# A scan-and-attention mixer: two drive steps set apart, one more PSUM bank in the ring, compressed scores by turns

## The chip, the cores and the metric

The kernel runs on one core of one Trainium2 chip. The metric is the time of one execution on the device, in microseconds (us). The engines are named as the profile names them: PE is TensorE's matmul (PEld its weight load), DVE is VectorE, ACT is ScalarE, POOL is GpSimd, SP is SyncE, which here only issues DMAs. L571 is line 571 of the kernel before.

## The reference

Two blocks over 512 tokens of width 1024, all in float32. The first block is an FFN, then a mixer, then a second FFN and a gated addition; the second block has two layers of its own, which the change leaves alone. The change lies in the mixer, and from one input projection the mixer makes two things:

```python
z = rmsnorm(h, norm_mix) @ w_in
q, kc, vc, ksl, vsl, kw, vw, g, u = split(z)
# attention, 8 heads in 2 groups, query blocks of 128
p_cmp = masked_softmax(q @ compress(kc).T * scale)     # 31 compressed keys
p_slc = masked_softmax(q @ ksl.T * scale)              # 8 blocks, all selected
p_win = masked_softmax(q @ kw.T * scale)               # window 512
o = g0 * (p_cmp @ vc') + g1 * (p_slc @ vsl) + g2 * (p_win @ vw)
# S5: 32 groups of 64 complex states, a linear recurrence over the 512 tokens
state[t] = a_bar * state[t-1] + b_coef * (B @ u[t])
y = gelu(Re(C @ state) + d * u);  out = y * sigmoid(y @ w_glu + b_glu)
h = h + concat(o, out) @ w_out
```

## The kernel before

Each engine runs its own program, in order, and semaphores join them. Activations lie transposed, with features on the 128 partitions and 512 tokens along the free dimension. Weights come by DMA from SP into three slots (`RAW`), in a fixed order in which a load waits until the tile three places ahead in that order has been used. Most weights are split in two halves: ACT writes the high one (`WHI`, L1109), DVE the low one (`WLO`, L1580), and PE multiplies three products.

**The mixer's order.** One generator, `mix_order` (L210), yields steps, and PE, ACT, DVE and POOL each walk the whole list and do their own part of a step. So one list sets the order on all of them. It goes through the four `u` projections, then eight `qk` projections with rotation (`rope`, `turn`) and the compression matmuls (`squeeze`), then eight `v` steps, then 34 rounds n of attention. In round n stand `values` of an earlier group, `flip` of scores n-2 (transposes, L785), `scale` of n-1, `scores` of n, for the first rounds also `squeeze` and `weigh`, and then two steps of the S5 generator `s5_order` (L191). In the `qk` part three S5 steps follow each projection, in the `v` part one.

**The S5 steps.** The 16 state tiles are worked in 8 batches b of two tiles j.
- `drive` b, j: PE makes the real and the imaginary input (two matmuls of 32 rows into two PSUM banks, L571); DVE makes four products with the rotation tables (L1796 to L1800; each has one PSUM input); POOL makes two additions (L2217, L2219).
- `scan` b, c, chunk c of 0 to 3: DVE runs four scans of 128 columns (L1816) and, between chunks, two small carry operations (L1821, L1823). The first scan needs POOL's additions of the drives of its batch.
- `back` b, j: one product on DVE (L1583) and three on POOL (L2230, L2232, L2234). They need the last scan of b, POOL's additions of `drive` b+1, j, since they write the same temporary buffers, and `read` b-1.
- `read` b: PE multiplies the eight results (L571, tiles of 32 columns), the last of them after POOL's last product of `back` b, 1; DVE adds into `U` (L1583, 64 partitions).

Before the change the order within a batch is: scans 0 to 3 of b, `read` b-1, `drive` b+1, 0, `drive` b+1, 1, `rest` (nothing), `back` b, 0, `back` b, 1.

**PSUM banks.** `take` pops the bank at the head of a list, `ring`, and makes PE wait until the last user of that bank has read it; `give` puts it at the tail with the name of that reader. Seven of the eight banks are in the ring; the eighth, `STAT`, is used only by `colsum`, the column sum of a normalization, of which the mixer's is read by DVE before the first `u` is stored. `squeeze` holds two banks over four steps, `v` four over eight, and `values` one over many rounds.

**Attention, each round.** PE writes two score tiles (one per key group, rows 0 to 63 and rows 64 to 127 of the array), DVE takes the row maximum (L1906), ACT the exponential (L1274), DVE the reciprocal and the gate (L1912, L1915), ACT the scaled copy (L1282), PE transposes (L785), ACT copies (L1290). `weigh` 0 to 3 are the compressed scores: per key group four matmuls of 31 columns with 64 rows (L571), and an addition of the mask on DVE (L1877). `weigh` 4 to 6 are their softmax.

Of the kernel before, what the change touches and what calls it, by code (L numbers as in the profile page):

```python
# [14 lines left out]
P = 128  # L15
# [175 lines left out]
def s5_order():  # L191
    for b in range(-1, 9):
        if 0 <= b < 8:
            for c in range(4):
                yield "scan", b, c
        if b >= 1:
            yield "read", b - 1
        if b + 1 < 8:
            yield "drive", b + 1, 0
            yield "drive", b + 1, 1  # L200
        if 0 <= b < 8:
            yield ("rest",)
            yield "back", b, 0
            yield "back", b, 1

# [90 lines left out]
def program(nc, D, out):  # L296
    ctx = ExitStack()
    with ctx:
# [78 lines left out]
        P_, A, V, G = Sig(sem("s_pe_done")), Sig(sem("s_act_done")), Sig(sem("s_dve_done")), Sig(sem("s_pool_done"))  # L377
# [6 lines left out]
        def loaded(name):  # L384
            if name not in X:
                X[name] = Sig(sem("s_" + name), 16)
            return X[name]
# [48 lines left out]
        ring = []  # L436

        def take(pe, *name):

            b, sig, by = ring.pop(0)  # L440
            if sig is not None:
                pe.wait_ge(*sig.at(*by))
            bank_of[name] = b
            return PS[b], b

        def give(b, sig, *by):
            ring.append((b, sig, by))
# [28 lines left out]
        Q = ar(13312, 4, T)  # L476
# [6 lines left out]
        KCC = ar(18816, 64)  # L483
# [82 lines left out]
        def pe_program(e):  # L566
            pe = PE(e)
            ring[:] = [(b, None, ()) for b in range(7)]

            def mm(o, l, r, start, stop):  # L570
                return pe.matmul(o, l, r, start=start, stop=stop, skip_group_check=True)  # L571
# [24 lines left out]
            def colsum(st):  # L596
                pe.wait_ge(*G.at("sq", st, 7))
                pe.wait_ge(*loaded("consts").at())
                mm(STAT[:, :], ONES, ACC, True, True).then_inc(*P_.up("colsum", st))

            def ffn(z):
# [45 lines left out]
            for step, *at_ in mix_order():  # L647
                if step == "u":
                    give(w_in(at_[0]), V, "u", at_[0])
                elif step == "rt":  # L650
                    ps, b = take(pe, "rt")
                    pe.wait_ge(*V.at("rs", "mix"))
                    for j in range(4):
                        t = pe.transpose(ps[:, P * j:P * j + P], RS[:, P * j:P * j + P], IDENT)
                    t.then_inc(*P_.up("rt"))
                    give(b, A, "rt")
                elif step == "drive":
                    b, j = at_
                    t16 = 2 * b + j
                    y4, r = t16 // 4, slice(32 * (t16 % 4), 32 * (t16 % 4) + 32)  # L660
# [8 lines left out]
                elif step == "read":  # L669
                    b, = at_  # L670
                    y4, r = b // 2, slice(64 * (b % 2), 64 * (b % 2) + 64)
                    ps, bY = take(pe, "read", b)
                    for z in range(4):
                        for j in range(2):
# [3 lines left out]
                            if z == 0:  # L678
                                pe.wait_ge(*V.at("back_im", t16))
                                t = mm(o, CpR[:, t16, :], S5T[k2], True, False)  # L680
                            elif z == 1:
                                pe.wait_ge(*G.at("back_re", t16))
                                t = mm(o, CpI[:, t16, :], S5T[k1], False, False)
                            elif z == 2:
                                pe.wait_ge(*G.at("back_vr", t16))
                                t = mm(o, CpR[:, t16, :], vr, False, False)
                            else:
                                pe.wait_ge(*G.at("back_vi", t16))
                                t = mm(o, CpI[:, t16, :], vi, False, True)
                    t.then_inc(*P_.up("read", b))  # L690
                    give(bY, V, "read", b)
                elif step == "qk":
                    i, = at_
                    b = w_in(4 + i)
                    give(b, V, *(("vct",) if i == 1 else ("rope", i)))
                elif step == "turn":
                    i, = at_
                    ps, b = take(pe, "turn", i)
# [3 lines left out]
                elif step == "squeeze":  # L702
                    z, c = at_
# [6 lines left out]
                    for mt in range(2):  # L710
                        for i in range(4):
                            ii = 4 * c + i
                            t = mm(hc_banks[z][mt][0][:, 0:62], w[:, i, P * mt:P * mt + P],
                                   XBp[:, ii, :, :].rearrange("p g c -> p (g c)"), ii == 0, ii == 15)
# [4 lines left out]
                elif step == "compressed":  # L719
                    z, = at_  # L720
                    ps, b = take(pe, "compressed", z)
                    pe.wait_ge(*A.at("hidc", z, 1))
                    pe.wait_ge(*loaded("small_w").at())
                    if z == 0:
                        for mt in range(2):
                            t = mm(ps[:, 0:62], WK2[:, mt, :], HIDc[:, mt, 0:62], mt == 0, mt == 1)
                    else:
                        for g in range(2):
                            for mt in range(2):
                                t = mm(ps[0:31, 64 * g:64 * g + 64], HIDc[:, mt, 31 * g:31 * g + 31], WV2[:, mt, :], mt == 0, mt == 1)  # L730
                    t.then_inc(*P_.up("compressed", z))
                    give(b, A, "compressed", z)
                elif step == "v":
# [6 lines left out]
                    for k in range(4):  # L740
# [6 lines left out]
                        t = mm(o, xl, hi[:, k, :], False, kk == 7)  # L747
# [4 lines left out]
                        give(v_banks[tt][1], A, "gx", tt)  # L752
                elif step == "weigh" and at_[0] < 4:
                    qt, = at_
                    for hf in range(2):
                        ps, b = take(pe, "weigh", qt, hf)
                        r = slice(64 * hf, 64 * hf + 64)
                        pe.wait_ge(*G.at("turn", 7))
                        pe.wait_ge(*A.at("compressed", 0))
                        for i in range(4):  # L760
                            t = mm(ps[:, 32 * i:32 * i + 31], Q[r, i, P * qt:P * qt + P], KCC[r, 31 * hf:31 * hf + 31], True, True)
                        t.then_inc(*P_.up("weigh", qt, hf))
                        give(b, V, "weigh", qt, hf)
                elif step == "scores":
                    i, kind, qt = at_
                    nk = P * (qt + 1)
                    keys = KSL if kind == 1 else KW
                    bs = [take(pe, "scores", i, kind, qt, hf) for hf in range(2)]
# [64 lines left out]
                    w_out(at_[0], (0, 1, 2), False, False)  # L833
            P_.name("mixed")
            P_.name("end", "mix")
            for m in range(KD):
                if m < 3:
                    w_out(m, (3,), False, True)
                else:
                    w_out_banks[m] = take(pe, "w_out", m)  # L840
                    w_out(m, (4, 5, 6, 7, 0, 1, 2, 3), True, True)
                give(w_out_banks[m][1], V, "h", "n2", m)
# [1645 lines left out]
```

## Time and profile before

| | before |
|---|---|
| median of 3 runs | 2070.99 us (2068.81 to 2073.7) |
| the profiled execution: its time | 2071.58 us |
| the profiled execution: its span | 2069.6 us |
| PE busy | 95% |
| DVE busy | 60% |
| ACT busy | 41% |
| POOL busy | 19% |
| mean granted clock of TensorE | 0.966 of full |
| mixer, from its first `u` weights to its last attention step | about 386 to 744 us of the span |

The page has parts: busy time of each engine, the span in 40 slices with the clock granted to TensorE (1.00 is 2.4 GHz, 0.50 is 1.2 GHz), the DMA queues, the chain of work that ended last, and the costliest groups. The trace behind it answers narrower questions: the time of each engine in given stretches, and single instructions in order of time, with the idle time ahead of each and whoever ended it. `x16` means 16 instructions of that form in one line; a float32 matmul shows as two instructions.

### The profile page before, as it was taken

Reading aid. Unit: us, or ns where it says so; the run is one execution under the profiler, and the core shown is the slowest. Engines: PE = TensorE matmul, PEld = TensorE weight load, DVE = VectorE, ACT = ScalarE, POOL = GpSimd, SP = SyncE. Lnnn points to the kernel's source line nnn. Section 1 sums busy time; section 2 is a strip of 40 time slices with the busy share of each in tenths; the row PEclk is TensorE's granted clock in tenths of the full one; section 3 lists DMA queues with packets and bytes.
Section 4 is the critical chain, followed back from the end, with each engine's and each line's share of the span. In section 5 each row is a group of like instructions: output and inputs, shape, how many; then the busy total and the mean of one; then the engine's idle time right before and its main releaser. Section 6 shows DMA issues by size and latency. Waiting matters only on the chain.

```text
span 2069.6 us, 21886 instructions
## 1 busy us (share of the span) xinstructions
PE 1972.3 (95%) x8614; PEld 1516.3 (73%) x8614; DVE 1246.1 (60%) x1646; ACT 846.8 (41%) x1269; POOL 387.6 (19%) x343
## 2 busy tenths in 40 slices
PE   7999999988977899999999999999999899999997
PEld 5888888766533478888888777776788778766786
DVE  6764344597697445665664776925773468536742
ACT  5231333201455633322333446645552357455531
POOL 2000000156254010100001202512400013214002
PEclk9999999998778899999999989999999999999998
DMA  5232232221000124554552222222122222220221
GB/s 187 89 127 81 92 112 93 86 67 68 26 0 1 67 82 163 198 198 151 195 200 75 82 91 79 82 82 82 52 92 93 94 86 82 91 82 31 92 92 61
DMA packets 53318, 196.69 MB, mean 95 GB/s; under 512 B 5985, under 2 KB 6497, under 8 KB 52705
## 3 DMA queue, kind: packets, MB, share of 16 engines
q1 hardware_dynamic: 43200, 160.55, 22.5%
q0 software_dynamic: 7504, 28.58, 4.2%
q10 hardware_dynamic: 2512, 6.18, 0.9%
q8 instruction: 68, 1.11, 0.2%
q14 instruction: 34, 0.27, 0.0%
HBM read 192.14 MB, written 2.10 MB: 94 GB/s over the span
## 4 chain that ended last, share of the span: by engine, by line
PE 77%; DVE 16%; ACT 3%; issue 1%; DMA 1%; POOL 1%; SPq 0%; POOLq 0%; DVEq 0%; ACTq 0%
PE PS L571 76%; DVE AR L1583 3%; DVE WLO L1580 2%; DVE AR L1816 2%; DVE AR L2065 1%; DVE AR L1906 1%; ACT WHI L1109 1%; DVE TMP L2139 1%; PE PS L785 1%; DVE AR L2032 0%; DMA RAW<-in_w13a 0%; DVE HNL L1583 0%; DVE AR L1862 0%; DMA RAW<-in_w_out 0%; DVE H L1968 0%
## 5 line engine op out<-in xcount | busy, mean ns | idle before, releaser
L1580 DVE TENSOR_TENSOR WLO<-RAW,WHI 128x1024 fp32r<-128x1024 f32 (+1 forms) x272 | 378.0, 1392 | 509.5 <-ACT WHI L1109 509.4
L571 PE MATMUL PS<-HNH,WHI 128*128 128x512 f32 x1632 | 657.8, 403 | 15.4 <-ACT HNH L1140 13.5
L571 PE MATMUL PS<-HNH,WLO 128*128 128x512 f32 x1632 | 640.5, 392 | 3.8 <-DVE WLO L1580 3.8
L1109 ACT ACTIVATE WHI<-RAW 128x1024 fp32r<-128x1024 f32 (+1 forms) x272 | 297.6, 1095 | 648.3 <-PE PS L571 577.0
L571 PE MATMUL PS<-HNL,WHI 128*128 128x512 f32 x1632 | 436.7, 390 | 0.4 <-DVE HNL L1583 0.2
L571 PEld LDWEIGHTS PS<-HNH,WHI 128*128 128x128 f32 x1632 | 308.6, 189 | 96.2 <-issue 22.1
L571 PEld LDWEIGHTS PS<-HNH,WLO 128*128 128x128 f32 x1632 | 308.9, 189 | 78.6 <-issue 9.1
L571 PEld LDWEIGHTS PS<-HNL,WHI 128*128 128x128 f32 x1632 | 307.3, 188 | 66.3 <-DVE HNL L1583 2.6
L2195 POOL TENSOR_TENSOR ACC<-ACC,SQ 128x512 f32<-128x512 f32 x46 | 62.8, 1366 | 782.3 <-ACT SQ L1124 781.3
L571 PE MATMUL PS<-AR 128*128 128x512 f32 (+12 forms) x652 | 184.0, 514 | 8.5 <-DVE SQ L1800 4.9
L571 PEld LDWEIGHTS PS<-AR 128*128 128x128 f32 (+5 forms) x652 | 87.8, 199 | 77.3 <-issue 48.4
L571 PE MATMUL PS<-HIDH,WHI 128*128 128x512 f32 x352 | 136.9, 389 | 0.0
L571 PE MATMUL PS<-HIDH,WLO 128*128 128x512 f32 x352 | 136.9, 389 | 0.0
L1583 DVE SCALAR_TENSOR_TENSOR AR<-AR,VEC 128x512 f32<-128x512 f32 x112 | 91.5, 817 | 3.7
L571 PE MATMUL PS<-HIDL,WHI 128*128 128x512 f32 x352 | 90.2, 389 | 0.0
L571 PEld LDWEIGHTS PS<-HIDH,WLO 128*128 128x128 f32 x352 | 66.1, 188 | 13.7
L571 PEld LDWEIGHTS PS<-HIDL,WHI 128*128 128x128 f32 x352 | 66.1, 188 | 13.7
L571 PEld LDWEIGHTS PS<-HIDH,WHI 128*128 128x128 f32 x352 | 66.1, 188 | 13.7
L2203 POOL DMA_DIRECT2D AR<-in_w_ada x48 | 25.4, 530 | 267.3 <-DVE MOD L1724 244.2
L1816 DVE TENSOR_TENSOR_SCAN AR<-AR 128x128 f32<-128x128 f32 x128 | 71.6, 620 | 0.8
L571 PE MATMUL PS<-YRH,WHI 128*128 128x512 f32 x192 | 69.8, 391 | 0.0
L1192 ACT ACTIVATE TMP<-TMP 128x512 f32<-128x512 f32 x44 | 27.8, 632 | 94.0 <-DVE TMP L1751 94.0
(314 smaller groups left out, 2465.0 us busy)
## 6 DMA issues: line engine op xcount, KB each, us to landing
RAW<-in_w_in SPq DMA_DIRECT2D x80, 512.0 KB, 3.5
AR<-in_w_ada POOLq DMA_DIRECT2D x48, 512.0 KB, 3.8
RAW<-in_w13a SPq DMA_DIRECT2D x44, 512.0 KB, 3.2
RAW<-in_w13b SPq DMA_DIRECT2D x44, 512.0 KB, 4.4
RAW<-in_w_out SPq DMA_DIRECT2D x40, 512.0 KB, 3.5
RAW<-in_w2a SPq DMA_DIRECT2D x16, 704.0 KB, 4.0
RAW<-in_w2b SPq DMA_DIRECT2D x16, 704.0 KB, 5.4
RAW<-in_w_inA SPq DMA_DIRECT2D x12, 512.0 KB, 3.2
```

Source lines behind the costliest of these rows:

```text
L571: return pe.matmul(o, l, r, start=start, stop=stop, skip_group_check=True)
L785: t = pe.transpose(ps[:, P * kb:P * kb + P], PB[:, u, P * kb:P * kb + P], IDENT)
L1109: act.activation(hi_of(name, i), raw_of(name, i), ACT.Copy).then_inc(*HI.up(name, i))
L1192: act.activation(TMP[:, q, :], TMP[:, q, :], ACT.Silu).then_inc(*A.up("silu", z, half, mi))
L1580: dve.tensor_tensor(lo_of(name, i), raw_of(name, i), f32(hi_of(name, i)), S_).then_inc(*LO.up(name, i))
L1583: return dve.scalar_tensor_tensor(out=o, in0=a, scalar=s, in1=b, op0=op0, op1=op1)
L1816: dve.tensor_tensor_scan(out=v, data0=rho, data1=v, initial=0.0 if c == 0 else E3[:, z, j:j + 1], op0=M_, op1=A_).then_inc(*V.up("scan", b ...
L1906: dve.tensor_reduce(ST[:, qt % 2, 0, hf:hf + 1], bank("scores", i, kind, qt, hf)[:, 0:P * (qt + 1)], AXX, ALU.max, negate=True).then_inc(* ...
L2065: dve.tensor_tensor_scan(out=CX[:, m, :], data0=RX[:, m, :], data1=IX[:, m, :], initial=0.0, op0=M_, op1=A_).then_inc(*V.up("rg_h", l, m))
L2139: dve.reciprocal(em, em).then_inc(*V.up("reciprocal", l, h))
L2195: pool.tensor_tensor(ACC, ACC, SQ[:, k % 2, :], A_).then_inc(*G.up("sq", st, k))
L2203: pool.dma_start(STMP[:, 1024 * (c % 2):1024 * (c % 2) + 1024], D["w_ada"][c]).then_inc(ada_sem[c % 2], 16)
```

## The change

Three edits. In `s5_order` the read of the batch before and the first drive of the next batch move ahead of chunks 2 and 3 of the scan, and the second drive stays behind them. In the mixer the bank of `STAT` joins the ring after `rt`, and is taken out again at the mixer's end, where the next `colsum` waits for its last reader. In `weigh` the two banks are taken first and the eight matmuls go by turns between the two key groups instead of four and four.

```diff
 def s5_order():
     for b in range(-1, 9):
         if 0 <= b < 8:
-            for c in range(4):
-                yield "scan", b, c
+            yield "scan", b, 0
+            yield "scan", b, 1
         if b >= 1:
             yield "read", b - 1
         if b + 1 < 8:
             yield "drive", b + 1, 0
+        if 0 <= b < 8:
+            yield "scan", b, 2
+            yield "scan", b, 3
+            yield ("rest",)
+        if b + 1 < 8:
             yield "drive", b + 1, 1
         if 0 <= b < 8:
-            yield ("rest",)
             yield "back", b, 0
             yield "back", b, 1
@@ colsum
                 pe.wait_ge(*loaded("consts").at())
+                if st == "n2":
+                    pe.wait_ge(*stat_free[0].at(*stat_free[1]))
@@ step rt
                     give(b, A, "rt")
+                    give(7, V, "ms", "mix")
@@ step weigh
-                    for hf in range(2):
-                        ps, b = take(pe, "weigh", qt, hf)
-                        r = slice(64 * hf, 64 * hf + 64)
-                        pe.wait_ge(*G.at("turn", 7))
-                        pe.wait_ge(*A.at("compressed", 0))
-                        for i in range(4):
-                            t = mm(ps[:, 32 * i:32 * i + 31], Q[r, i, P * qt:P * qt + P], KCC[r, 31 * hf:31 * hf + 31], True, True)
-                        t.then_inc(*P_.up("weigh", qt, hf))
+                    bs = [take(pe, "weigh", qt, hf) for hf in range(2)]
+                    pe.wait_ge(*G.at("turn", 7))
+                    pe.wait_ge(*A.at("compressed", 0))
+                    ts = {}
+                    for i in range(4):
+                        for hf, (ps, b) in enumerate(bs):
+                            r = slice(64 * hf, 64 * hf + 64)
+                            ts[hf] = mm(ps[:, 32 * i:32 * i + 31], Q[r, i, P * qt:P * qt + P], KCC[r, 31 * hf:31 * hf + 31], True, True)
+                    for hf, (ps, b) in enumerate(bs):
+                        ts[hf].then_inc(*P_.up("weigh", qt, hf))
                         give(b, V, "weigh", qt, hf)
@@ end of the mixer
             P_.name("end", "mix")
+            stat_free = next(r for r in ring if r[0] == 7)[1:]
+            ring[:] = [r for r in ring if r[0] != 7]
```

## Rows read from the trace of the kernel before

**Rows 1.** The page, part 1: busy time, share of the span, instructions.
```profile
PE 1972.3 (95%) x8614; PEld 1516.3 (73%) x8614; DVE 1246.1 (60%) x1646; ACT 846.8 (41%) x1269; POOL 387.6 (19%) x343
```

**Rows 2.** Six stretches: length, busy time by engine, granted clock, DMA share, GB/s.
```profile
446.00:487.00 41.00, 41.00 (x179) 27.27 (x179) 29.99 (x48) 6.02 (x7) 24.40 (x18) 0.88 0.33 113
487.00:518.00 31.00, 25.23 (x118) 18.81 (x116) 27.59 (x41) 2.33 (x8) 18.78 (x14) 0.78 0.07 25
532.00:566.00 34.00, 33.30 (x164) 23.01 (x166) 18.14 (x51) 14.47 (x35) 9.64 (x8) 0.57 0.05 17
566.00:588.00 22.00, 14.53 (x69) 7.26 (x68) 19.24 (x31) 10.55 (x27) 11.21 (x9) 0.71 0.00 0
588.00:664.00 76.00, 61.23 (x306) 25.50 (x305) 65.37 (x149) 40.28 (x116) 36.17 (x27) 0.88 0.00 1
...
548.00:564.00 16.00, 16.00 (x77) 10.43 (x77) 11.66 (x35) 7.23 (x19) 1.31 (x1) 0.50 0.02 6
```

**Rows 3.** Timeline of PE, `qk` 4 to `drive` 2: start, length, what, [idle before].
```profile
434.84 0.80 PE L571 MATMUL PS<-HNH,WHI 128*128 128x512 f32 x1
...
440.73 1.02 PE L571 MATMUL PS<-TMP,CONST 128*128 128x512 f32 x2
445.55 3.65 PE L571 MATMUL PS<-AR,RAW 128*128 128x62 f32 x16 [3.80 <-DVE AR L1862]
...
452.45 3.79 PE L571 MATMUL PS<-AR 128*32 128x512 f32 x12
```

**Rows 4.** Timelines of POOL and SP in the same place.
```profile
445.01 1.49 POOL L2234 TENSOR_TENSOR AR<-AR 128x512 f32<-128x512 f32 x1
...
449.23 0.33 SPq L2337 DMA_DIRECT2D RAW<-in_w_inA  x1
```

**Rows 5.** Timelines of PE and DVE in the `v` steps.
```profile
491.57 0.57 PE L571 MATMUL PS<-WHI,HNH 128*128 128x280 f32 x1 [4.50 <-DVE TMP L1853]
...
504.16 0.69 DVE L1796 TENSOR_TENSOR AR<-PS,AR 128x512 f32<-128x512 f32 x1 [0.85 <-PE PS L571]
505.87 0.69 DVE L1798 TENSOR_TENSOR RS<-PS,AR 128x512 f32<-128x512 f32 x1 [1.02 <-PE PS L571]
...
509.66 1.75 DVE L1583 SCALAR_TENSOR_TENSOR ACC<-AR 128x512 f32<-128x512 f32 x1 [1.17 <-POOL AR L2219]
```

**Rows 6.** Timeline of PE in rounds 2 and 3.
```profile
530.30 0.33 PE L785 MATMUL PS<-CONST,HX 128*128 128x128 f32 x1 [1.71 <-DVE SQ L1800]
532.70 1.65 PE L571 MATMUL PS<-AR 64*128 64x384 f32 x4 [2.06 <-DVE ACC L1800]
...
538.01 2.79 PE L571 MATMUL PS<-AR 64*128 64x31 f32 x16
...
546.12 1.55 PE L571 MATMUL PS<-AR 64*128 64x31 f32 x16
```

**Rows 7.** Timeline of DVE in rounds 2 to 6.
```profile
539.97 0.29 DVE L1877 TENSOR_TENSOR AR<-PS,CONST 128x124 f32<-128x124 f32 x1 [4.15 <-PE PS L571]
...
565.97 0.75 DVE L1583 SCALAR_TENSOR_TENSOR AR<-AR,VEC,PS 64x512 f32<-64x512 f32 x1 [4.25 <-PE PS L571]
...
568.99 1.22 DVE L1906 TENSOR_REDUCE AR<-PS 128x1 f32<-128x384 f32 x2 [1.87 <-PE PS L571]
```

**Rows 8.** Scans: three by form while POOL works (640.5 to 643.9), four alone.
```profile
L1816 DVE TENSOR_TENSOR_SCAN AR<-AR 128x128 f32<-128x128 f32 x3 | 4.2, 1438 | 0.0
...
646.80 1.61 DVE L1816 TENSOR_TENSOR_SCAN AR<-AR 128x128 f32<-128x128 f32 x4
```

**Rows 9.** Timelines: POOL's first operation of a batch, and DVE after the drives.
```profile
630.33 1.27 POOL L2217 TENSOR_TENSOR AR<-AR,SQ 128x512 f32<-128x512 f32 x1 [13.42 <-DVE SQ L1798]
...
611.38 0.95 DVE L1906 TENSOR_REDUCE AR<-PS 128x1 f32<-128x256 f32 x2 [1.37 <-PE PS L571]
...
638.02 1.22 DVE L1906 TENSOR_REDUCE AR<-PS 128x1 f32<-128x384 f32 x2 [1.02 <-PE PS L571]
```

**Rows 10.** Timeline of PE: scores of 128 columns, which already go by turns.
```profile
667.22 0.49 PE L571 MATMUL PS<-AR 64*128 64x128 f32 x4
```

## The prediction

> **What bounds the kernel now.** I read the page first: PE is busy 95% of the span [rows 1], but only the mixer is touched, so the page's average says little. The second view is the busy time by stretch [rows 2]. It shows five regimes. From 446 to 487 PE has no gap at all. From 487 to 518 PE and DVE take turns at being late. From 532 to 566 PE is full again, but at a granted clock of 0.57, that is mostly at 1.2 GHz, and DVE is busy for 18.14 of 34 us. From 566 to 664 DVE is the bound: 19.24 of 22 us, then 65.37 of 76. After that no S5 step is left, and the order is untouched. The third view is the timeline of each engine in those places, for the waits that end last. The rest of the span, some 1,700 us of FFNs and second block, keeps its instructions and its order, so a shift in the mixer passes through to the end one for one.
>
> **Part 1: read 0 goes ahead of qk 4.** The new order doesn't only part the drives. It also puts each read two scans earlier. In the `qk` part three S5 steps follow a projection, and there read 0 moves from behind the first squeeze to ahead of `qk` 4. Today PE runs `qk` 4 from 434.84 to 440.73, waits 3.80 us for the positions, squeezes from 445.55, then reads and drives until 452.45 + 3.79 = 456.24 [rows 3]. Read 0 needs POOL's last product of back 0, 1, which ends at 445.01 + 1.49 = 446.50 [rows 4]; POOL and DVE have the same work ahead of it in both orders, so I leave that time. Then in the changed kernel: read ends about 447.6 (one more pair of matmuls); `qk` 4 takes 5.9 us and about 1 more, since PE has idled and will start at the lower clock, 454.5; turn 3 takes 1.0, 455.5; the squeeze 1.8 at the full clock (half of 3.65), 457.3; the drive 1.0, 458.3. That is 2.1 us later than 456.24. PE has no gap for 31 us after that, so it counts: **+2.1**, bounds 0 (a later wait swallows it) to +5. Queued behind that wait are the squeeze and, behind the squeeze, SP's load of the next `w_inA` tile, issued at 449.23 today [rows 4], which would go out at about 457.4 instead. Its tile is needed by `qk` 6 at about 466, so I cost it at nothing; the cover is `qk` 5 and squeeze 1, some 8 us.
>
> **Part 2: the v steps.** Drive 3, 0 now stands ahead of `v` 0 and is done on PE before the wait of 4.50 us for turn 5 [rows 5]. That wait stays, with eight banks as with seven, because the four banks of `v` still include the one that turn 5 frees. The two gaps of DVE for the late drive 3, 1 (0.85 and 1.02) and the one for POOL's addition (1.17) sum to 3.04 us [rows 5]. I take them as gone, less 0.9 for scan 2, 3, which will now meet POOL's addition of turn 6: **-2.1**, bounds -4.5 (PE's wait as well) to 0.
>
> **Part 3: the bank waits of rounds 2 to 7.** Two waits of PE are for a bank that the pair of drives holds: 1.71 for the flip and 2.06 for the scores [rows 6]. With bank 7 and with the drives apart, the flip of round 2 takes a bank of an exponential and the scores those of a drive two rounds old: both waits go, 3.8 us. What is late next is the scale that the flip transposes. It follows DVE's round 0, which now has a drive (four products of 0.6, [rows 5]) and a scan with its carry (2.0, and 1.25 for POOL, see part 5) where it had a scan and the read; so the flip starts some 0.8 us later than today, the scores start at about 529.5 instead of 532.7, and drive 4, 1 (2 us at the lower clock) has to be fitted in behind. PE is then 1.2 us ahead. DVE gets drive 5, 0 only after that round's scores, weigh and drive on PE, and has its own 1.25 more. I take **-0.5**. The nearest rows bound it: DVE's three large gaps in this stretch and just behind it are 4.15, 4.25 and 1.87 [rows 7], -10.3 if all were to go; +3 if DVE waits for drive 5, 0 at the lower clock.
>
> **Part 4: compressed scores by turns.** Sixteen instructions take 2.79 us at 1.2 GHz and 1.55 at full clock, 97 ns each [rows 6]. Score matmuls of 128 columns that already alternate take 0.49 for four, 122 ns each [rows 10]; so with 31 columns there is little left to overlap. Bounds: nothing, or half, if the two row groups ran fully side by side (1.4 and 0.8 us a step). The alternated row is nearer to the lower end, so 0.3 us for each of four steps; three of them lie where PE is the bound: **-1.0**, bounds -4.5 to 0. The Trainium skill, "TensorEngine Tiling (Array Packing)", section Key Properties, says that different tiles can load weights and multiply in parallel. By it this part would be about half of each step, -4.5, and the whole sum 3.5 us lower. No run here has yet shown weight loads of 31-column matmuls side by side.
>
> **Part 5: the batches where DVE is the bound.** A scan alone takes 1.61 / 4 = 0.40 us; while POOL works it takes 1.44 [rows 8]. Drives don't pay this: each product has a PSUM input. Today POOL's ten operations of a batch start at 630.33 [rows 9] and run without a gap, some 1.3 us each, the first under the drives, the last under the backs and the first scan chunk. In the changed order the second addition of drive b+1, 0 starts just as DVE goes on to scan chunk 2: one scan waits for one POOL operation, +1.25 for each batch. POOL's tail after the second drive is as long as today, but DVE reaches the next chunk 0 one attention round sooner, so more of that chunk is slow: +0.5. Against it stand DVE's gaps in the round after the pair, when PE is late with scores because their flip waited on a long round of DVE: 1.87 [rows 7], 1.37 and 1.02 [rows 9]; rounds are more even, and I take all three as gone. Three pairs: 3.75 + 1.5 - 4.26 = **+1.0**, bounds -4.3 to +6. The Trainium skill, "SBUF — State Buffer", section Who interferes with whom, says that an operation of DVE with two SBUF inputs is blocked for the whole of a GpSimd operation that reads SBUF, and one with a single SBUF input isn't. By it the +1.25 is certain and a carry or gate operation can pay it too, which would add about 1 a batch and make the sum 3 us higher; the rows agree on scans and drives.
>
> **What costs nothing.** Read 1 to 7 move ahead of a drive on PE; they fill time in which PE waits for a scale today. The wait added to `colsum` asks for a reader of the mixer's last steps and comes after the first two FFN tiles, each about as long as the 5.9 us of `qk` 4. After 664 the order is unchanged.
>
> **The sum.** 2.1 - 2.1 - 0.5 - 1.0 + 1.0 = -0.5. The profiled execution took 2071.58 us, of which 2069.6 are its span; the median of the runs is 0.59 lower. So 2071.1 against the profile and **2070.5** against the median.
>
> **The rivals.**
> *A, the forecast (0.46).* The terms cancel; 2066.9 to 2075.1.
> *B, the clock comes back (0.33).* Between 532 and 566 PE is full at 1.2 GHz after it had waited since 528. If removing 3.8 us of waits keeps the clock at 2.4 GHz there, the same instructions take about 0.56 of their time (1.55 for 2.79, [rows 6]); of 34 us, most at the lower clock, PE saves up to 13, and DVE with 34 - 18.14 = 15.9 us of free time lets most of it through: I take 8 us, 2062.5 to 2063. For it: the stretch follows directly on the bank waits. Against it: the flip must still wait for the scale, about 3 us of idle PE; and from 548 to 564 PE is busy without a gap and the clock is still 0.50 [rows 2].
> *C, the read stalls the projections (0.13).* The price of part 1 is 5 rather than 2 us. Its place is PE's in-order queue: `qk` 4, the squeeze and then the load and its two splits stand behind POOL's last product. DVE asks for the low half right behind turn 3, at about 456, and the load is issued at 457.4 and lands 3.7 later: DVE stands still for some 5 us. It decides from the point at which DVE, not PE, is late for turn 5 at 491; then part 2's gain is gone as well: -0.5 + 3 + 2 + 1 = +5.5, 2076.5.
> *D, POOL in the way (0.08).* Every operation that DVE moves next to a POOL addition pays. At 2.5 us for each of drives 4 to 7 instead of 1.25, with no gap regained (4.3 in part 5): +9, 2079.5.
>
> **Chances.** What can be told from no change here is about 0.2%, 4.1 us. Faster 0.33 (B), same 0.46 (A), slower 0.21 (C and D). The range takes in A and the sizes of B and C: 2062 to 2078; B at its full 13 us and D lie outside.
>
> **What would show it.** Part 1: PE idle between about 434 and 446 and `qk` 4 after read 0; `w_inA` load near 457. Part 2: no DVE gap ahead of drive 3, 1. Part 3: no wait on L1800 products by PE in rounds 2 and 3, and the clock of 532 to 566: above 0.8 means B. Part 4: sixteen 31-column instructions in 2.5 us (1.2 GHz) or 1.25. Part 5: the first scan of chunk 2 near 1.4 us, and batches 24 to 27 us apart as today. The prediction is wrong if the time from 532 to 588 changes by more than 4 us, or the start of `v` by more than 5.

## The result, and the profile after

| | before | after |
|---|---|---|
| median | 2070.7 us (2068.8 to 2073.7) | 2084.9 us (2082.5 to 2085.8) |
| ratio, 95% interval | | 1.0064 [1.0051, 1.0077] |
| span of the profiled execution | 2069.6 us | 2083.9 us |

The change makes the kernel 13.3 us slower by the ratio (0.64% of 2071 us). That is outside the range of the prediction (2062 to 2078) and on the other side of its likeliest case.

The page of the changed kernel, busy time by engine, against [rows 1]: PE is busy 18 us longer and DVE 10, with the same number of instructions.

```profile
PE 1990.3 (96%) x8614; PEld 1516.1 (73%) x8614; DVE 1256.1 (60%) x1646; ACT 846.4 (41%) x1269; POOL 390.9 (19%) x343
```

The stretches of [rows 2] in the changed kernel (length, then busy time of PE, its weight loads, DVE, ACT and POOL, granted clock, DMA share, GB/s):

```profile
446.00:487.00 41.00, 41.00 (x186) 29.78 (x184) 27.18 (x45) 6.01 (x7) 21.29 (x16) 0.94 0.29 96
487.00:518.00 31.00, 26.37 (x133) 17.05 (x129) 29.43 (x45) 5.65 (x12) 19.61 (x15) 0.94 0.13 48
532.00:566.00 34.00, 34.00 (x169) 21.65 (x166) 18.69 (x47) 14.30 (x36) 10.47 (x8) 0.58 0.06 16
566.00:588.00 22.00, 14.81 (x62) 6.96 (x60) 20.73 (x39) 9.93 (x27) 8.49 (x7) 0.69 0.00 1
588.00:664.00 76.00, 64.25 (x260) 25.25 (x260) 64.93 (x129) 34.52 (x97) 33.58 (x24) 0.79 0.00 1
```

From 532 to 566 the clock is what it was (0.58, was 0.57): rival B did not come. From 588 to 664 it is lower than before (0.79, was 0.88), PE is busy 3 us longer, and less is done in it: 129 instructions of DVE instead of 149. The time was lost there. The best ruler for it is the start of each attention round's first row maximum on DVE (L1906 before, L1917 after). Its 32 rounds carry the same steps of attention in both kernels, and the last `read` stands in round 22 in both. In a table, in us between the starts:

| rounds | 0 to 3 | 3 to 8 | 8 to 13 | 13 to 18 | 18 to 23 | 0 to 23 |
|---|---|---|---|---|---|---|
| before | 21.7 | 39.8 | 27.5 | 26.6 | 28.4 | 144.0 |
| after | 23.6 | 39.0 | 31.8 | 34.4 | 29.2 | 158.0 |

The sum is 14.0 us longer, the span 14.3. The second block and the FFNs pass it on one for one, as predicted. A caution for single profiles: the changed kernel and an experiment that has the same code up to there (e_fill) reach round 0 at 522.5 and 525.0 us, so positions are good to 2.5 us only, and I compare lengths within one profile.

PE of the changed kernel in rounds 11 to 12 and 15 to 18:

```profile
607.32 1.03 PE L794 MATMUL PS<-CONST,HX 128*128 128x128 f32 x6 [2.33 <-ACT HX L1293]
...
609.34 3.77 PE L575 MATMUL PS<-AR 32*128 32x512 f32 x4
...
628.83 1.98 PE L575 MATMUL PS<-AR 32*128 32x512 f32 x4
...
638.32 1.94 PE L794 MATMUL PS<-CONST,HX 128*128 128x128 f32 x8 [5.25 <-ACT HX L1293]
640.19 1.23 PE L575 MATMUL PS<-AR 64*128 64x256 f32 x4
641.35 0.39 PE L575 MATMUL PS<-MASK 128*128 128x128 bf16 x2
641.67 3.78 PE L575 MATMUL PS<-AR 32*128 32x512 f32 x4
```

The rows of `32*128` are drives. A first drive (628.83) takes 1.98 us, and so does drive 5, 1 (at 574.66). The second drives of batches 6 and 7 (609.34, 641.67) take 3.77 and 3.78: PE has stood 2.33 and 5.25 us waiting for a scale, and the granted clock behind that is 0.52 (608 to 616) and 0.50 (636 to 648). DVE at the same time:

```profile
603.28 2.58 DVE L1827 TENSOR_TENSOR_SCAN AR<-AR 128x128 f32<-128x128 f32 x4
...
611.44 0.69 DVE L1807 TENSOR_TENSOR AR<-PS,AR 128x512 f32<-128x512 f32 x1 [0.64 <-PE PS L575]
613.15 0.69 DVE L1809 TENSOR_TENSOR RS<-PS,AR 128x512 f32<-128x512 f32 x1 [1.02 <-PE PS L575]
...
618.56 5.51 DVE L1827 TENSOR_TENSOR_SCAN AR<-AR 128x128 f32<-128x128 f32 x4
624.11 1.05 DVE L1832 TENSOR_TENSOR AR<-AR 128x8 f32<-128x8 f32 x1
...
641.67 0.95 DVE L1917 TENSOR_REDUCE AR<-PS 128x1 f32<-128x256 f32 x2 [1.57 <-PE PS L575]
643.78 0.69 DVE L1807 TENSOR_TENSOR AR<-PS,AR 128x512 f32<-128x512 f32 x1 [1.16 <-PE PS L575]
645.49 0.69 DVE L1809 TENSOR_TENSOR RS<-PS,AR 128x512 f32<-128x512 f32 x1 [1.01 <-PE PS L575]
...
651.35 1.22 DVE L1917 TENSOR_REDUCE AR<-PS 128x1 f32<-128x384 f32 x2 [2.13 <-PE PS L575]
```

Two things are to be seen. DVE waits for the second drive. And its scans are longer: chunk 2, behind the first drive, 2.58 (1.61 before), chunk 0 of batch 5 4.49 (2.39 before), that of batch 6 5.51 (4.48 before), its carry 1.05 (0.17). Chunk 0 of batch 7 takes 4.50, as before (4.48).

### The profile page after: what moved, and what is told of

Read it like the earlier page. It is cut to its first block, busy times and chain, and to the rows that moved or that the text cites. A ratio compares the mean times of both kernels' runs of the same rounds, so it can differ in the third digit from the quotient of the medians.

```text
span 2083.9 us, 21883 instructions
## 1 busy us (share of the span) xinstructions
PE 1990.3 (96%) x8614; PEld 1516.1 (73%) x8614; DVE 1256.1 (60%) x1646; ACT 846.4 (41%) x1269; POOL 390.9 (19%) x343
## 4 chain that ended last, share of the span: by engine, by line
PE 76%; DVE 16%; ACT 4%; POOL 2%; issue 2%; DMA 1%; SPq 0%; POOLq 0%; DVEq 0%; ACTq 0%
PE PS L575 75%; DVE AR L1594 3%; DVE WLO L1591 3%; DVE AR L1827 2%; DVE AR L2076 1%; ACT WHI L1120 1%; PE PS L794 1%; DVE TMP L2150 1%; DVE AR L1917 1%; DVE AR L2043 0%; DVE HNL L1594 0%; DMA RAW<-in_w13a 0%; DVE H L1979 0%; DVE AR L1926 0%; POOL ACC L2326 0%
## 5 line engine op out<-in xcount | busy, mean ns | idle before, releaser
L575 PE MATMUL PS<-AR 128*128 128x512 f32 (+11 forms) x652 | 201.9, 523 | 2.8 <-POOL AR L2245 1.1
L575 PEld LDWEIGHTS PS<-AR 128*128 128x128 f32 (+4 forms) x652 | 89.2, 201 | 78.1 <-issue 45.2
L1827 DVE TENSOR_TENSOR_SCAN AR<-AR 128x128 f32<-128x128 f32 x128 | 78.8, 676 | 0.8
L1203 ACT ACTIVATE TMP<-TMP 128x512 f32<-128x512 f32 x44 | 27.8, 632 | 94.1 <-DVE TMP L1762 94.1
```

Source lines behind the costliest of these rows:

```text
L1203: act.activation(TMP[:, q, :], TMP[:, q, :], ACT.Silu).then_inc(*A.up("silu", z, half, mi))
L1827: dve.tensor_tensor_scan(out=v, data0=rho, data1=v, initial=0.0 if c == 0 else E3[:, z, j:j + 1], op0=M_, op1=A_).then_inc(*V.up("scan", b ...
```

## The experiments

In all, a ratio is to the kernel before on the same chip, with its 95% interval, and us are the ratio's distance from 1 times 2071. A +- behind a difference of two runs is worked out from both intervals.

### Which part of the change costs it

**e_order**: the new `s5_order` alone. Against the changed kernel:

```diff
-                    give(7, V, "ms", "mix")
...
-                    bs = [take(pe, "weigh", qt, hf) for hf in range(2)]
+                    for hf in range(2):
+                        ps, b = take(pe, "weigh", qt, hf)
...
```

> The kernel before with the new order of the S5 steps alone: seven banks, compressed scores as before. Theory O (the order costs it: the second drive of a batch now stands in a round of its own, behind that round's scores on PE, and after a light round): the whole loss is here, +12 to +18 us against before, since without the eighth bank the two bank waits of rounds 2 and 3 come on top. Rival R (the eighth bank turns the ring so that PE meets other readers, and the order is harmless): within 4 us of before.

Measured 2093.0 us, ratio 1.0106 [1.0093, 1.0119], +22.0 us. The order alone costs more than the whole change, even more than theory O said.

**e_bank_weigh**: the other edits without the new order. **e_bank**: of these the bank alone. Against the kernel before, the first line is in both, the second in e_bank_weigh only:

```diff
+                    give(7, V, "ms", "mix")
...
+                    bs = [take(pe, "weigh", qt, hf) for hf in range(2)]
...
```

> The kernel before with the eighth bank in the ring and the compressed scores by turns, the S5 order as before. Theory O: these two are gains or nothing, -1 to -5 us (the bank waits of 1.71 and 2.06 go, and up to 1 us in weigh). Rival R: here is the loss, +10 or more.

> The kernel before with the eighth bank in the ring alone. With compressed scores by turns as well it took 2064.6. Theory: the bank waits of 1.71 and 2.06 go and pass through only in part: -2 to -5 us against before, 2065 to 2068. Rival: the gain of the pair is all in the compressed scores (half of four steps, 4.5 us): then within 1.5 us of before.

Measured 2064.6 us, 0.9975 [0.9964, 0.9987], -5.2 us, and 2065.8 us, 0.9971 [0.9959, 0.9982], -6.0 us. So the eighth bank is a gain of about 6 us, and the compressed scores by turns add nothing that can be measured, although the step itself is shorter. PE in rounds 2 and 3 of e_bank, then of e_bank_weigh:

```profile
529.73 0.92 PE L571 MATMUL PS<-AR 64*128 64x384 f32 x4 [1.60 <-DVE SQ L1805]
534.32 2.79 PE L571 MATMUL PS<-AR 64*128 64x31 f32 x16
```

```profile
531.69 0.92 PE L571 MATMUL PS<-AR 64*128 64x384 f32 x4 [1.60 <-DVE SQ L1807]
536.21 1.92 PE L571 MATMUL PS<-AR 64*128 64x31 f32 x16
```

In the old order one wait of 1.60 us for a drive's bank is left where there were two, 1.71 and 2.06 [rows 6]. The 16 matmuls take 1.92 us instead of 2.79 at the lower clock. Where the 0.87 us of a step went isn't shown. In the two profiles e_bank_weigh is 1.9 us shorter than e_bank from round 0 to 8 and 2.8 longer from 22 to 23. But its profiled execution took 2070.9 us, 6 above its median, and that of e_bank 2062.7, 3 below.

**e_late** and **e_early**: the whole change, with the new order only from batch 3 on (attention), or only up to batch 2 (`qk` and `v` steps). The eighth bank enters the ring three places ahead of the tail, so that it is free at the mixer's end. The diff is that of e_late; e_early has `b < 3`.

```diff
+        apart = b >= 3
-            yield "scan", b, 0
-            yield "scan", b, 1
+            for c in range(2 if apart else 4):
+                yield "scan", b, c
...
-        if 0 <= b < 8:
+        if apart and 0 <= b < 8:
             yield "scan", b, 2
...
-                    give(7, V, "ms", "mix")
+                    ring.insert(5, (7, V, ("ms", "mix")))
```

> The changed kernel, but with the new order of the S5 steps only from batch 3 on, that is in the attention rounds; the qk and v steps have the old order. Theory O: the loss is all in the rounds from 564 us on, +11 to +14 us. Rival E (the 2 to 3 us by which turn 5 is late in the qk and v steps set off the rest, by another phase of PE against DVE): 0 to +4.

> The changed kernel, but with the new order of the S5 steps only up to batch 2, that is in the qk and v steps; the attention rounds have the old order. Theory O: the early part costs 1.6 us (scan 3, 0 starts 1.6 us later in the changed kernel) and the bank and the compressed scores give 1 to 4 back: -3 to +1 us. Rival E: +10 to +14.

Measured 2084.1 us, 1.0064 [1.0052, 1.0076], and 2068.0 us, 0.9988 [0.9979, 0.9997]. So the new order costs 2.7 us (+-3.0) in the `qk` and `v` steps (e_early less e_bank_weigh), and 15.7 (+-3.3) in attention (the changed kernel less e_early). With the -5.2 of the other edits these make 13.2, and 13.3 was measured. This is one way to divide the loss: e_late, without the early part, is as slow as the changed kernel, so there the early part costs nothing and the late one 18.4. From here on only the 15.7 us are looked for, and e_early is what the changed kernel is compared with. Its eighth bank stands at another place of the ring; so does that of e_late, which still takes the changed kernel's time.

### What in the late order costs it

PE can be one round ahead of DVE at most: `flip` n-2 needs `scale` n-2, whose gate DVE makes at the start of its round n-1. So while DVE is in round n-1, PE does flip, scores and drive of round n. DVE's S5 steps by round, in the order before: chunks 1 and 2; chunk 3 and read; both drives; first back; second back and chunk 0. In the changed order: first drive and chunk 2 (5.0 to 5.4 us); chunk 3 alone (1.6); second drive and first back; second back and chunk 0; chunk 1 and read.

**e_pe_early**: PE makes the matmuls of the second drive at the step `rest`, a round before DVE's products.

```diff
-            yield ("rest",)
+            yield "rest", b
...
+                if step == "drive" and at_[1] and at_[0] > 3:
+                    give(held.pop(0), V, "drive", 2 * at_[0] + 1)
+                    give(held.pop(0), V, "drive_im", 2 * at_[0] + 1)
+                    continue
+                if step == "rest" and 3 <= at_[0] < 7:
+                    step, at_ = "drive", (at_[0] + 1, 1)
+                    held.append(None)
...
+                    if held:
+                        held[:] = [bR, bI]
+                        continue
```

> The changed kernel, but from drive 4, 1 on PE makes the two matmuls of the second drive at the step rest, one round sooner than DVE's products; DVE, POOL and the order of all else as in the changed kernel, the two banks held until their old place. Theory L (the second drive stands too late in PE's queue, behind the scores and the flip of its round, and DVE waits for it: 0.64, 1.02 and 1.16, 1.01 us, and PE has lost its clock): 5 to 9 us back of the 14, to about 2077. Rival U (the rounds are uneven on DVE, it is not PE's place that counts): within 2 us of the changed kernel, 2083 to 2087.

Measured 2080.8 us, 1.0043 [1.0031, 1.0056]: 4.3 us back (+-3.7). That lies between what theory L said and what U allowed, and the interval reaches both: PE's place alone is a part of the loss, by the interval at most about half.

**e_rest** and **e_rest7**: from batch 3 on the empty step comes behind the first drive. The diff is that of e_rest7, where batch 7 is left as it was; in e_rest it moves too.

```diff
             yield "drive", b + 1, 0
...
+            if 3 <= b < 7:
+                yield "rest", b
             yield "scan", b, 2
             yield "scan", b, 3
-            yield ("rest",)
+            if not 3 <= b < 7:
+                yield "rest", b
```

> The changed kernel, but from batch 3 on the empty step stands behind drive b+1, 0 instead of behind scan b, 3. So a round with a drive and a scan (5.4 us on DVE) and one with a scan alone (1.6) become one with a drive (2.8) and one with two scans (4). The second drive stays where it is. Theory U (a heavy round followed by a light one makes the engines wait for each other in turn): 5 to 10 us back, 2075 to 2080. Theory L: within 2 us of the changed kernel, less the 0.96 for each blocked scan if POOL is done by then: 2081 to 2086.

> e_rest, but batch 7 keeps its old rounds (in e_rest they went one step later and the round 22 to 23 took 12.2 us instead of 8.1 to 9.8). Theory U (what counts is that the round ahead of the second drive is long enough for PE to do its flip, scores and drive in it): 2 to 5 us below e_rest's 2078. If the tail was no matter: 2078.

Measured 2078.0 us, 1.0032 [1.0020, 1.0045], and 2078.6 us, 1.0034 [1.0020, 1.0047]: 6.2 to 6.6 us back (+-3.9), in the range of theory U; the tail of batch 7 is no matter, against what I expected. But the edit also parts chunk 2 from POOL's addition (1.61 us instead of 2.58), which the next run prices, so not all of it is the length of rounds. Rounds 0 to 3 take 15.8 us in e_rest7 (23.6 in the changed kernel) and 13 to 18 27.7 (34.4).

**e_thin**: POOL's second addition of each first drive from batch 4 on is done on 8 columns.

```diff
+                    n = 8 if b > 3 and j == 0 else T
-                    pool.tensor_tensor(vi, vi, S5T[k2], S_).then_inc(*G.up("drive_im", t16))
+                    pool.tensor_tensor(vi[:, 0:n], vi[:, 0:n], S5T[k2][:, 0:n], S_).then_inc(*G.up("drive_im", t16))
```

> The changed kernel, but POOL's second addition of drive b, 0, from b = 4 on, is done on 8 columns instead of 512 (that part of the computation is left out), so that the scan of chunk 2 meets no POOL operation. Theory D (POOL in the way of DVE is what costs the late batches): 8 us or more back, below 2077. Theories L and U: the four blocked scans give 0.96 each at most, 1 to 4 back, 2081 to 2084; the gaps of DVE in front of the second drive stay.

Measured 2081.3 us, 1.0051 [1.0038, 1.0063]: 2.7 us back (+-3.7), so not clear of noise, and far from the 8 of theory D. The one blocked scan of a batch is not the loss.

**e_pool_new** and **e_pool_old**: all five POOL operations of a state tile so shortened from drive 4 and back 3 on, in the new and in the old order. The cut shows one of the five.

```diff
+                    n = 8 if b > 2 else P
...
-                    pool.tensor_tensor(f4(vr), f4(vr), c4, M_).then_inc(*G.up("back_vr", t16))
+                    pool.tensor_tensor(f4(vr)[:, :, 0:n], f4(vr)[:, :, 0:n], c4[:, :, 0:n], M_).then_inc(*G.up("back_vr", t16))
...
```

> The changed kernel, with all five POOL operations of a state tile shortened to 8 of 512 (or 128) columns from drive 4 and back 3 on; that part of the computation is left out. To be read against e_pool_old, which has the old order there. With whole POOL operations the pair is 2084.9 against 2068.0, 16.9 apart. Theory D2 (DVE is busy 11 us longer over rounds 8 to 22 because its scans, carries and backs meet more of POOL's operations, and most of the loss is that): the pair comes to 3 to 8 us apart. Rival W (the loss is waiting between PE and DVE): still 12 or more apart.

> The kernel of e_early (eighth bank, compressed scores by turns, old order of the S5 steps from batch 3 on), with the same POOL operations shortened; that part of the computation is left out. Each chunk 0 of batches 6 and 7 takes 4.48 us instead of 1.61 in e_bank, those of 4 and 5 less: by D2 the whole is 5 to 10 us below e_early's 2068; by W within 3 of it.

Measured 2065.2 us, 0.9980 [0.9967, 0.9992], and 2054.9 us, 0.9924 [0.9909, 0.9939]: 11.6 us apart (+-4.0), with whole operations 15.7. Between both expectations, nearer to W; the 4.1 us between the pairs are not clear of noise. The traces show why they are no more. DVE over rounds 3 to 23:

| | DVE busy | idle, ended by PE | length |
|---|---|---|---|
| e_early | 99.3 | 15.3 | 121.7 |
| changed kernel | 108.0 | 18.9 | 134.4 |
| e_pool_old | 83.6 | 17.8 | 107.6 |
| e_pool_new | 84.3 | 25.2 | 116.0 |

With whole POOL operations the new order makes DVE's work 8.7 us longer and its waits for PE 3.6. With short ones its work is 0.7 longer and its waits 7.4. So nearly all of the added work is POOL's doing, and removing it lets DVE arrive sooner and wait for PE instead. Of the 8.7 us the scans are 6.0; the gates and the carries, operations of 2 and 8 columns, are 1.8. DVE of e_pool_new behind round 16:

```profile
627.17 0.95 DVE L1917 TENSOR_REDUCE AR<-PS 128x1 f32<-128x256 f32 x2 [1.57 <-PE PS L575]
629.28 0.69 DVE L1807 TENSOR_TENSOR AR<-PS,AR 128x512 f32<-128x512 f32 x1 [1.15 <-PE PS L575]
630.98 0.69 DVE L1809 TENSOR_TENSOR RS<-PS,AR 128x512 f32<-128x512 f32 x1 [1.01 <-PE PS L575]
637.26 1.22 DVE L1917 TENSOR_REDUCE AR<-PS 128x1 f32<-128x384 f32 x2 [3.51 <-PE PS L575]
```

The same four waits as in the changed kernel stand there (1.57, 1.16, 1.01, 2.13), the last one longer.

**e_backs_old** and **e_backs_new**: the empty step behind both backs from batch 3 on, in e_bank and in the changed kernel.

```diff
-            yield ("rest",)
+            if b < 3:
+                yield ("rest",)
             yield "back", b, 0
             yield "back", b, 1
+            if b >= 3:
+                yield ("rest",)
```

The diff is that of e_backs_old; in the changed kernel the empty step is taken from behind scan b, 3.

> The kernel of e_bank (the kernel before with the eighth bank alone), but from batch 3 on the empty step stands behind the two backs instead of ahead of them: back b, 0 and back b, 1 share a round, and chunk 0 of the next batch comes one step later, when POOL has done more of its products. By D2: chunk 0 near 2 us instead of 4.48 in batches 6 and 7, 3 to 6 us below e_bank's 2065.8. By W: the round of the backs is longer and the next shorter, 0 to 4 us above e_bank.

> The changed kernel with the empty step behind the two backs from batch 3 on, so scan b, 3 and drive b+1, 1 share a round and chunk 0 follows POOL's tail at a distance. By D2: chunk 0 falls from 5.5 to about 2 us and 6 to 10 us come back, 2075 to 2079; the blocked scan of chunk 2 stays. By W: 0 to 4 us back.

Measured 2065.0 us, 0.9969 [0.9957, 0.9980], and 2072.7 us, 1.0006 [0.9995, 1.0017]. The first is as fast as e_bank (2065.8) and tells nothing about POOL: the scans of rounds 8 to 23 sum to 25.8 us in both, so the edit did not take them out of its way. In the second they fall from 30.9 to 26.8, and 12.0 us (+-3.5) come back, more than D2 said. But the edit does two things: the second drive also moves into the round behind the long one. So it can't say how much each gave.

**e_fill**: PE works where it waited, on matmuls that nobody reads.

```diff
-            yield ("rest",)
+            yield "rest", b
...
+                elif step == "rest" and at_[0] in (5, 6):
+                    b, sig, by = ring[0]
+                    pe.wait_ge(*sig.at(*by))
+                    for _ in range(2 if at_[0] == 5 else 5):
+                        mm(PS[b][:, :], IDENT, Q[:, 0, :], True, True)
```

> The changed kernel, but PE, where it waits 2.33 and 5.25 us for a scale in rounds 11 and 16, makes matmuls of 512 columns whose result nobody reads (2 and 5 of them, about 1 us each at the full clock), in the bank that it would take next anyway. Nothing else is changed. Theory C (the idle time costs PE its clock, and the second drives behind it take 3.77 us instead of 1.98): the clock of 608 to 616 and of 636 to 648 is 1.0 instead of 0.5, the second drives take 2 us, and 3 to 6 us come back. Rival W2 (PE is late because the flip waits for the scale, at whatever clock): less than 2 us, or a loss where the filling itself delays the flip.

Measured 2084.0 us, 1.0064 [1.0053, 1.0076]: nothing back. Its PE in round 16 and 17, and the stretch 636 to 648:

```profile
633.44 4.56 PE L575 MATMUL PS<-AR,CONST 128*128 128x512 f32 x10
638.97 1.33 PE L799 MATMUL PS<-CONST,HX 128*128 128x128 f32 x8 [0.97 <-ACT HX L1298]
...
641.09 1.98 PE L575 MATMUL PS<-AR 32*128 32x512 f32 x4
```

```profile
636.00:648.00 12.00, 10.98 (x56) 4.99 (x55) 10.48 (x26) 7.13 (x21) 4.59 (x4) 1.00 0.01 1
```

The filling did what it should: the clock there is 1.00 (0.50 in the changed kernel) and the second drive takes 1.98 us. Rounds 8 to 18 shrink from 66.2 us to 59.5. But rounds 18 to 23 grow from 29.2 to 32.5, and the median does not move. The profile of e_late, which has the same order here and no filling, is a second reading of this. PE waits as long, and yet drive 7, 1 takes 2.00 us:

```profile
634.07 1.94 PE L797 MATMUL PS<-CONST,HX 128*128 128x128 f32 x8 [5.57 <-ACT HX L1296]
...
637.42 2.00 PE L578 MATMUL PS<-AR 32*128 32x512 f32 x4
```

Its rounds 18 to 23 take 32.5 us as well, and its median (2084.1) is that of the changed kernel. So the lost clock is a delay at its place that later rounds take up. At these two drives it can be 3.6 of the 15.7 us at most, by both intervals; at drive 4, 1 in round 2 it was not tested alone.

**e_both** and **e_pool_both**: e_rest7 with PE's matmuls as in e_pe_early, and that with POOL's operations shortened. The edits are those of the diffs above, taken together.

> e_rest7, and in addition PE makes both drives of a batch in one round as in the kernel before, while DVE takes them two rounds apart. If the wait for PE is all that is left beside POOL, this comes to within 6 us of e_early (2068): 2070 to 2074. If PE's place is already no matter once the round ahead is long: as e_rest7, within 2.

> e_both with POOL's operations shortened as in e_pool_new (that part of the computation is left out). If light rounds, PE's place and POOL are the whole of it, this is within 3 us of e_pool_old (2054.9). If it stays 6 or more above, something in the order is not accounted for.

Measured 2073.6 us, 1.0012 [1.0002, 1.0022], and 2053.4 us, 0.9913 [0.9897, 0.9929]. The last is 2.3 us (+-4.5) below e_pool_old by the ratios (0.9924). So the account closes, as well as these runs can tell. With long enough rounds and PE's matmuls early, 10.8 (+-3.4) of the 15.7 us are gone; the 5.0 (+-2.8) that stay go when POOL is shortened in both. Stretch by stretch it is less neat: e_pool_both is 2.6 us shorter than e_pool_old in rounds 0 to 3 and 4.4 longer in 3 to 8. The length of the rounds, in us, in all of these (the profiled execution of e_rest7 took 2074.7, 4 us below its median):

| rounds | 0 to 3 | 3 to 8 | 8 to 13 | 13 to 18 | 18 to 23 | 0 to 23 |
|---|---|---|---|---|---|---|
| e_early | 17.3 | 39.2 | 27.4 | 26.3 | 28.8 | 139.0 |
| changed kernel | 23.6 | 39.0 | 31.8 | 34.4 | 29.2 | 158.0 |
| e_rest7 | 15.8 | 39.4 | 29.5 | 27.7 | 32.4 | 144.8 |
| e_both | 15.6 | 35.8 | 31.8 | 28.0 | 32.4 | 143.7 |
| e_pool_old | 17.3 | 33.2 | 26.0 | 24.2 | 24.2 | 124.9 |
| e_pool_new | 22.1 | 34.8 | 26.7 | 30.8 | 23.7 | 138.2 |
| e_pool_both | 14.7 | 37.6 | 27.8 | 24.5 | 23.7 | 128.4 |

## Why the prediction was wrong

The sum had the terms +2.1, -2.1, -0.5, -1.0 and +1.0. Measured by their runs they are +2.7 (+-3.0) for the first two together, -5.2 (+-2.4) for the next two, and +15.7 (+-3.3) for the last, with what the order costs in rounds 0 to 3.

**Part 1 held, and its last digit is luck.** PE waits 1.20 and 3.72 us in read 0, `qk` 4 follows it, the drive ends at 458.3 (predicted 458.3), and the load is issued at 456.37 (457.4). I had `qk` 4 and turn 3 at 7.9 us, with 1 for the lower clock, and they took 6.6; I had the drive at 1.0, and it took 1.99. PE and SP of the changed kernel:

```profile
442.84 1.06 PE L575 MATMUL PS<-RS,AR 128*32 128x512 f32 x1 [3.72 <-POOL RS L2241]
...
456.27 1.99 PE L575 MATMUL PS<-AR 32*128 32x512 f32 x4
```

```profile
456.37 0.33 SPq L2348 DMA_DIRECT2D RAW<-in_w_inA  x1
```

DVE reaches the low half of `w_inV` 0 at 481.87 instead of 479.95, +1.9. Rival C's wait of DVE for that load is there too (5.43 us at 460.77), but by then only 1.9 us of it are left.

**Part 2 was too good.** The gaps of 0.85 and 1.02 [rows 5] are gone, the one of 1.17 is still there (1.19), and the four scans of batch 2 take 11.4 us together instead of 9.9, where I had added 0.9 for one of them:

```profile
485.28 4.50 DVE L1827 TENSOR_TENSOR_SCAN AR<-AR 128x128 f32<-128x128 f32 x4
...
497.99 2.59 DVE L1827 TENSOR_TENSOR_SCAN AR<-AR 128x128 f32<-128x128 f32 x4
...
503.57 2.71 DVE L1827 TENSOR_TENSOR_SCAN AR<-AR 128x128 f32<-128x128 f32 x4
...
511.25 1.76 DVE L1594 SCALAR_TENSOR_TENSOR ACC<-AR 128x512 f32<-128x512 f32 x1 [1.19 <-POOL AR L2230]
```

Scan 3, 0 starts 1.6 us late, so part 2 gave -0.3 instead of -2.1.

**Part 3 had the right mechanism and the wrong size.** The wait for the bank is gone in the changed kernel, and the flip waits for the scale, as predicted; but the scores start at 531.33, where I had 529.5:

```profile
530.72 0.67 PE L794 MATMUL PS<-CONST,HX 128*128 128x128 f32 x2 [2.17 <-ACT HX L1293]
...
536.65 5.63 PE L575 MATMUL PS<-AR 64*128 64x31 f32 x20
```

In the old order the bank is worth 6 us. In the new order it is worth more (22.0 less 13.3, with the compressed scores). But I mis-sized what came behind. I put drive 4, 1 at "2 us at the lower clock", which is what a drive takes at the full one, the same error as in part 1. The row of 536.65 holds its four instructions with the 16 of `weigh`: 5.63 less 1.92 is 3.7. DVE waits for it, and round 3 starts 12.9 us after round 2 (9.5 before). For that loss I had a bound of +3; rounds 0 to 3 are 6.3 us longer than in e_early.

**Part 4**: 16 instructions by turns take 1.92 us at 1.2 GHz, where I had 2.5 from the alternated 128-column row. For the time of the kernel it made no difference that can be measured: -6.0 us without it, -5.2 with it. By the Trainium skill, "TensorEngine Tiling (Array Packing)", section Key Properties, different tiles can load weights and multiply in parallel; my estimate by that was half of 2.79, 1.4. The measurement stands between the two.

**Part 5 is the step that failed.** I wrote that "rounds are more even, and I take all three as gone". I never listed DVE's steps by round. The list in the section above shows the opposite: the round with the first drive and chunk 2 (7.0 us in batch 6) is as long as the one with two drives was (6.6), and the next holds one chunk. Under that next round of 3.5 us PE must do flip, scores and second drive, which took it 5.8 us (607.32 to 613.11). One batch later they took 7.1 (638.32 to 645.45) under a round of 4.1. In the order before, the second drive stood behind the first in PE's queue and was made under DVE's products of the first. The gaps that I took as gone (1.87, 1.37, 1.02) came back as 1.57, 1.16, 1.01 and 2.13 in one batch. The bounds of the term were made from DVE's gaps alone and left PE's place out, so its upper end, +6, had nothing of this. Measured, DVE's waits for PE are 3.6 us longer than in e_early over rounds 3 to 23, and 7.4 once POOL is out of the way.

**POOL, rival D, was in the sum at about its size, but split wrongly.** I had 3.75 + 1.5, and gave 0.08 to a price of 9. Shortening POOL narrows the distance of the orders by 4.1 us in one pair of runs and by 7.3 in the other (each +-5), so its share is known only roughly. Chunk 2 cost 0.97 us a batch, where I had 1.25. Too low was the tail: POOL's products run on into chunk 0 (4.49 us instead of 2.39 in batch 5, 5.51 instead of 4.48 in batch 6) and one carry. The Trainium skill, "SBUF — State Buffer", section Who interferes with whom, says that an operation of DVE with two SBUF inputs contends with one of GpSimd that reads SBUF. The trace agrees for small operations: a carry takes 1.05 instead of 0.17, and a gate took 1.01 (at 635.99 us) already in the kernel before. I had named the rule and kept them out of the sum; in rounds 3 to 23 they make 1.8 us.

## What to carry to other kernels

In a pipeline in which one engine can run only one round ahead of another, write down what each engine has in each round before and after a change of order. An operation of the engine ahead (here PE) that comes to stand behind a short round is no longer hidden under the other engine's work, and here the clock that PE had lost in its wait made it longer still. A cause that is removed alone (here POOL's operations or the clock) gives back only a part, since the next wait takes its place; only when the candidates were removed together did the account close. And time the parts of a change separately: here one edit that gains 6 us (one more bank) was hidden under one that loses 18. The best versions are the kernel before with the eighth bank alone, 2065.8 us, or with the compressed scores too, 2064.6; the runs can't tell them apart.

## What the runs showed of the hardware

- The two matmuls of a drive (32 rows, 512 columns, four instructions) take 1.98 us at a granted clock of 1.00 and 3.77 at 0.50.
- The eight matmuls of `weigh` (64 rows, 31 columns, 16 instructions) take 2.79 us in the order four and four, and 1.92 when they alternate between the two halves of the rows, both at 0.50.
- While POOL works, a scan of 128 columns takes up to 1.4 us instead of 0.4, an operation on 8 columns with SBUF inputs 1.05 instead of 0.17, and one on 2 columns 1.03 instead of 0.16 (DVE at 615.85 us of the changed kernel):

```profile
615.85 1.03 DVE L1926 TENSOR_TENSOR AR<-AR 128x2 f32<-128x2 f32 x1
```
